# A hybrid decoder trunk on one core: a ring of split weights of four units instead of three, from the first pair of experts on

## The chip, the core and the metric

One core of a Trainium2 chip runs the whole kernel. The metric is the device time of one execution in microseconds (us). TensorE (PE) multiplies, VectorE (DVE) and ScalarE (ACT) work on elements, GpSimd (POOL) has small work, SyncE (SP) issues the loads.

## What is computed

Two decoder layers over 256 tokens of width 1024, in float32. Layer 0 has differential attention, a dense SwiGLU of width 2816 and a gated per-layer embedding. Layer 1 has a pooling mixer, a mixture of eight experts of width 3584 with two experts to a token, and again a gated embedding. The part around the change is the experts:

```python
def swiglu(xn, w_gate, w_up, w_down):
    return (jax.nn.silu(xn @ w_gate) * (xn @ w_up)) @ w_down

def moe_swiglu(xn, w_router, w_gate, w_up, w_down):
    logits = (xn @ w_router).astype(jnp.float32)
    top_v, top_i = lax.top_k(logits, TOP_K)
    top_w = jax.nn.softmax(top_v, axis=-1)
    gates = jnp.sum(jax.nn.one_hot(top_i, N_EXPERTS, dtype=jnp.float32) * top_w[..., None], axis=-2)
    out = jnp.zeros_like(xn)
    for e in range(N_EXPERTS):
        ye = swiglu(xn, w_gate[e], w_up[e], w_down[e])
        out = out + gates[..., e:e + 1].astype(xn.dtype) * ye
    return out
```

The weights of the eight experts are 336 of some 400 units of 1 MiB that the kernel reads.

## The kernel before, in words

**Units.** All weights pass through the core in units of 128 partitions by 2048 float32 (`UNIT`, 1 MiB), counted by one index u. A product in float32 is made of three products in the format fp32r: each weight and each activation is split in a high part (rounded copy) and a low part (rest), and high x high, high x low and low x high are summed (`product`, L342). So a unit goes through four steps:

- SP loads it into one of `RAW` = 7 slots of `raw` (`load`, L331, with the transfer at L340). The load of unit u waits until DVE has split the unit that had the slot, u-7.
- ACT writes the high part into `w_hi` (`split_hi`, L290; the copy is L307). It waits for the landing, and for `unit_used`: PE must have given back the unit that had the same slot of the ring of split weights. `SPLIT` = 3, so unit u waits for u-3.
- DVE writes the low part into `w_lo` (`split_lo`, L309; L324) after ACT, and counts `lo_ready`.
- PE waits for `lo_ready` and multiplies; its last matmul counts `unit_used`.

Each engine runs a list of instructions written out by hand, in order. At step n of a block ACT and DVE issue the split of unit u + n + `AHEAD` (2), and around it the block's small work: the silu (L1521), the high part of the hidden rows (L1526, L1529), its low part (L2076, L2079), the results (`result_hi`, `result_lo`, L2304), their addition to the residual (L2313) and the gathering of tokens for the next experts (`gather_piece` on PE, L1092).

**The expert stage.** The first expert runs alone (`first_turn`, units 56 to 95). Then come pairs of experts (`pair`, unit index from `U_PAIR`), three pairs for these inputs, the third in a loop over a register; then the last expert alone (`last_turn`), its last two down units, and the second layer's embedding gate. Each pair has seven blocks f of 512 hidden columns, and in each block twelve units: two gate, two up and two down units of the one expert, e = 0, and the same of the other, e = 1. Expert e = 0 has at most 64 tokens (`few`): its up and down units take 8 matmuls (`product_few`, L1111 and L1112), all others 12 (L344 to L346). In the first two blocks of a pair results of experts before are scattered and added; in the last one the next experts' tokens are gathered. Twelve units begin with one fold of hidden rows (L929); the stretch from one to the next is called a period here.

**Counting over the turns.** The pair loop reuses the same unit indices: `PER_EXPERT` = 42 units per expert are added as `PER_EXPERT * k` to each wait. 42 and 84 are divisible by 3 and by 7, so slots are the same in each round.

**Space.** Two units of the first expert (87 and 88, `EXTRA`) are loaded ahead into `extra_raw`, outside the ring of `raw`, over the space of an earlier stage. After they have been split this space lies idle.

Of the kernel before, what the change touches and what calls it, by code (L numbers as in the profile page):

```python
# [29 lines left out]
P = 128  # L30
# [41 lines left out]
EXTRA_TURNS = 10  # L72
U_PAIR = U_TURN - 2


def trunk(nc, dram):
    ctx = ExitStack()
    with ctx:
# [14 lines left out]
        with nc.sbuf_tensor("wide", [P, 6144], F32) as wide:  # L93
            pass
        extra_raw = sb("extra_raw", [P, EXTRA * UNIT])
        xb = sb("xb", [P, 2 * D], F32R)
# [171 lines left out]
        def raw_slot(u):  # L268
# [3 lines left out]
            return raw[:, ring(u) % RAW, :]  # L272

        def load_wait(eng, u, k=0):

            if in_wide(u):
                eng.wait_ge(extra_landed[u - U_WIDE], 16)
            else:
                eng.wait_ge(landed[ring(u) % RAW], 16 * (ring(u) // RAW + 1) + 16 * (PER_EXPERT // RAW) * k)

# [9 lines left out]
        def split_hi(u, k=0, by=None):  # L290

            load_wait(nc.scalar, u, k)
            if u == U_POOL:
                nc.scalar.wait_ge(mixer_scaled, 2)
            if u >= SPLIT:
                nc.scalar.wait_ge(unit_used, u - SPLIT + 1 + PER_EXPERT * k)
            if by is not None:
                n, c0 = by
                nc.scalar.wait_ge(gain_cols_landed, 16 * len(COLUMNS))
                for c in range(KD if u == U_POOL else 4):  # L300
                    width = 256 if u == U_POOL else 512
                    cols = slice(width * c, width * c + width)
                    last = nc.scalar.activation(w_hi[:, u % SPLIT, cols], raw_slot(u)[:, cols], ACT.Copy,
                                                scale=column(n, c0 + c))
                last.then_inc(hi_ready, 1)
                return
            nc.scalar.activation(w_hi[:, u % SPLIT, :], raw_slot(u), ACT.Copy).then_inc(hi_ready, 1)  # L307

        def split_lo(u, k=0, by=None):  # L309

            nc.vector.wait_ge(hi_ready, u + 1 + PER_EXPERT * k)
            if by is not None:
                n, c0 = by
                nc.vector.wait_ge(gain_cols_landed, 16 * len(COLUMNS))
                for c in range(KD if u == U_POOL else 4):
                    width = 256 if u == U_POOL else 512
                    cols = slice(width * c, width * c + width)
                    last = nc.vector.scalar_tensor_tensor(out=w_lo[:, u % SPLIT, cols], in0=raw_slot(u)[:, cols],
                                                          scalar=column(n, c0 + c),
                                                          in1=w_hi[:, u % SPLIT, cols].bitcast(F32),  # L320
                                                          op0=ALU.mult, op1=ALU.subtract)
                last.then_inc(lo_ready, 1)
                return
            nc.vector.tensor_tensor(w_lo[:, u % SPLIT, :], raw_slot(u), w_hi[:, u % SPLIT, :].bitcast(F32),  # L324
                                    ALU.subtract).then_inc(lo_ready, 1)

        def split_wait(eng, u, k=0):

            eng.wait_ge(lo_ready, u + 1 + PER_EXPERT * k)
# [18 lines left out]
        def weights(u, c, n0, n, width):  # L348

            at = c * width + n0  # L350
            return w_hi[:, u % SPLIT, at:at + n], w_lo[:, u % SPLIT, at:at + n]

# [9 lines left out]
        def _(sp):  # L362
# [154 lines left out]
            for half, view in enumerate(down_views(e, FB - 1)):  # L517
                load(sp, U_TURN + half, view, turns)
            load_ple(1, U_TURN + 2, turns)

# [114 lines left out]
        def _(pe):  # L635
# [635 lines left out]
            for half in range(2):  # L1271
                down(U_TURN + half, FB - 1, half, JF + FB - 1, 1, turns, end=half == 1, h_t=(a_hi, a_lo))

# [11 lines left out]
            def next_part():  # L1285

                return project_part(1, *next(parts), U_TURN + 2)

            unit(U_TURN + 2, turns)
            next_part()  # L1290
# [12 lines left out]
            last.then_inc(unit_used, 1)  # L1303
            gates(1, U_TURN + 3, turns)


        @block.scalar
        def _(act):
            def used(u, k=0):

                act.wait_ge(unit_used, u + 1 + PER_EXPERT * k)

# [412 lines left out]
            turns = extra + (NE - 1)  # L1725
            pairs = act.value_load(more[0:1, 1:2], min_val=0, max_val=EXTRA_TURNS // 2) + 3
            pair(0, first=True)
            pair(2)
            with act.Fori(3, pairs + 1) as it:
                pair((it - 1) * 2)  # L1730
            last_turn(turns - 1)
            split_hi(U_TURN + AHEAD, turns)
            for n in range(2):
                if n == 0:
                    act.wait_ge(y_half, 1)
                else:
                    used(U_TURN + 1, turns)
                nc.scalar.activation(y_hi[:, 512 * n:512 * n + 512], ps[:, 3 + n, :], ACT.Copy).then_inc(y_hi_ready, 1)

            split_hi(U_TURN + 1 + AHEAD, turns, by=(5, 0))  # L1740
            transposed_hi(5)
            split_hi(U_TURN + 2 + AHEAD, turns, by=(5, 4))
            square_norm(5, turns)
            split_hi(U_TURN + 3 + AHEAD, turns, by=(5, 0))
            split_hi(U_TURN + 4 + AHEAD, turns, by=(5, 4))
            sigmoids(1, 0, U_TURN + 4, turns)
            sigmoids(1, 1, U_TURN + 6, turns, tiles=(0,))
            act.wait_ge(resid_ready, 18)
            for h, bank in enumerate((GATE_BANKS[1][3], GATE_BANKS[1][0])):
                used(U_TURN + 5 + h, turns)  # L1750
                nc.scalar.activation(sig[1][:, 256 * h:256 * h + 256], ps[:, bank, 0:256], ACT.Sigmoid,
# [4 lines left out]
        def _(dve):  # L1756
# [8 lines left out]
            def used(u, k=0):  # L1765

                dve.wait_ge(unit_used, u + 1 + PER_EXPERT * k)

# [607 lines left out]
            def pair(k, slots, first=False):  # L2376

                for f, e in PAIR_BLOCKS:
                    g, u = block_at_seq(f, e), pair_unit(f, e, first)
                    bare = first and f == 0 and e == 0  # L2380
                    for n in range(4 if bare else 6):
                        split_lo(u + n + AHEAD, k)
                        if f == 0 and e == 1 and n == 0 and not first:
# [23 lines left out]
            def last_turn(k):  # L2407

                for f in range(FB):
                    g, u = JF + FB + f, last_unit(f)  # L2410
                    for n in range(6 if f else 8):
                        split_lo(u + n + AHEAD, k)
                        if f == 0 and n == 6:
# [16 lines left out]
            turns = extra + (NE - 1)  # L2430
            pairs = dve.value_load(more[0:1, 1:2], min_val=0, max_val=EXTRA_TURNS // 2) + 3
            pair(0, iota_few[:, :], first=True)
# [4 lines left out]
            split_lo(U_TURN + AHEAD, turns)  # L2437
            for n in range(2):
# [17 lines left out]
            transposed_lo(5, (0,))  # L2456
            split_lo(U_TURN + 1 + AHEAD, turns, by=(5, 0))
            transposed_lo(5, (1, 2, 3))
            split_lo(U_TURN + 2 + AHEAD, turns, by=(5, 4))
            norm_mean(5, 0)  # L2460
            norm_mean(5, 1)
            split_lo(U_TURN + 3 + AHEAD, turns, by=(5, 0))
            split_lo(U_TURN + 4 + AHEAD, turns, by=(5, 4))
            add_gated(1, 0)
# [158 lines left out]
```

## Time and profile before

| | us |
|---|---|
| median of 3 runs | 1371.45 (1371.35 to 1371.47) |
| the profiled execution | 1370.36 |
| its span in the trace | 1368.6 |
| PE busy | 1323.0 |
| DVE busy | 1155.5 |
| ACT busy | 951.6 |

Between the span and the time of the profiled execution lie 1.76 us. The granted clock of TensorE is 1.00 throughout. A matmul of 512 columns is shown with 0.39 us, while the next one starts 0.23 us after it: ends are modelled and overlap, so short idle times of PE do not show in its busy time. PEld is PE's weight load. POOL's spans are rough, and its work here is small. "DMA share" in the windows can be a little above 1 where the packets of an engine overlap.

### The profile page before, as it was taken

What the parts mean: (1) busy time and instruction counts of PE and PEld (TensorE: products, weight loads), DVE (VectorE), ACT (ScalarE), POOL (GpSimd) and SP (SyncE); (2) the same over time, 40 slices, a digit from 0 to 9 for tenths busy, and PEclk for the clock granted to TensorE, in tenths of its full rate; (3) what the DMA queues carried; (4) which work ended last, traced back from release to release, by engine and by line L of the source; (5) the groups of instructions that cost most, each with busy time, mean ns of one, the idle gap of its engine ahead of it and who ended that gap; (6) DMA issues with size and microseconds to landing.
All of it is one profiled execution on the core that took longest, in us unless ns stands there. A gap on an engine that the chain in (4) does not pass through costs nothing.

```text
span 1368.6 us, 17326 instructions
## 1 busy us (share of the span) xinstructions
PE 1323.0 (97%) x6404; PEld 1082.3 (79%) x6404; DVE 1155.5 (84%) x963; ACT 951.6 (70%) x879; POOL 72.3 (5%) x133
## 2 busy tenths in 40 slices
PE   8999999999999999999999999999999999999998
PEld 7776888888877887777777777777777777778887
DVE  6897655556889989999989999898999898899886
ACT  5676544446776777777777777777777777777775
POOL 2120920000200000000000000000000000000000
PEclk9999999999999999999999999999999999999999
DMA  8743765555299899999999999999999999999980
GB/s 302 265 133 92 252 204 193 184 185 166 81 363 335 306 341 359 366 390 394 379 388 354 346 381 382 392 381 391 357 359 362 385 393 389 336 395 368 354 311 31
DMA packets 197860, 422.46 MB, mean 309 GB/s; under 512 B 13064, under 2 KB 37392, under 8 KB 197776
## 3 DMA queue, kind: packets, MB, share of 16 engines
q1 hardware_dynamic: 197776, 421.35, 84.8%
q8 instruction: 52, 0.85, 0.2%
q14 instruction: 32, 0.26, 0.1%
HBM read 420.27 MB, written 1.05 MB: 308 GB/s over the span
## 4 chain that ended last, share of the span: by engine, by line
PE 76%; DVE 15%; ACT 5%; issue 2%; SPq 1%; DMA 1%; POOL 0%; ACTq 0%; DVEq 0%; POOLq 0%
PE ps L344 20%; PE ps L346 19%; PE ps L345 19%; DVE w_lo L324 11%; PE ps L952 5%; ACT w_hi L307 4%; PE ps L950 3%; PE ps L929 1%; PE ps L1092 1%; PE ps L932 1%; PE ps L1105 1%; PE ps L949 1%; PE ps L1111 1%; DMA raw<-in_attn_w_qkv_dram 1%; PE ps L1112 1%
## 5 line engine op out<-in xcount | busy, mean ns | idle before, releaser
L324 DVE TENSOR_TENSOR w_lo<-raw,w_hi 128x2048 fp32r<-128x2048 f32 x382 | 871.1, 2290 | 128.8 <-ACT w_hi L307 125.6
L307 ACT ACTIVATE w_hi<-raw 128x2048 fp32r<-128x2048 f32 x385 | 734.9, 1916 | 223.2 <-PE ps L346 203.6
L344 PE MATMUL ps<-w_hi,xe 128*128 128x512 f32 x392 | 156.3, 399 | 1.7 <-DVE w_lo L324 1.5
L346 PE MATMUL ps<-w_hi,xe 128*128 128x512 f32 x392 | 153.1, 391 | 0.0
L345 PE MATMUL ps<-w_lo,xe 128*128 128x512 f32 x392 | 152.8, 390 | 0.0
L344 PE MATMUL ps<-w_hi,h_t_hi 128*128 128x512 f32 x360 | 141.0, 392 | 2.2 <-DVE w_lo L324 2.2
L345 PE MATMUL ps<-w_lo,h_t_hi 128*128 128x512 f32 x360 | 140.2, 390 | 0.0
L346 PE MATMUL ps<-w_hi,h_t_lo 128*128 128x512 f32 x360 | 140.2, 389 | 0.0
L344 PE MATMUL ps<-w_hi,xb 128*128 128x512 f32 x336 | 135.2, 402 | 4.1 <-DVE w_lo L324 3.5
L346 PE MATMUL ps<-w_hi,xb 128*128 128x512 f32 x336 | 131.3, 391 | 0.0
L345 PE MATMUL ps<-w_lo,xb 128*128 128x512 f32 x336 | 131.0, 390 | 0.0
L952 PE MATMUL ps<-a_all,w_hi 128*128 128x512 f32 x308 | 109.8, 396 | 0.0
L950 PE MATMUL ps<-a_all,w_lo 128*128 128x256 f32 x352 | 90.9, 279 | 0.0
L2507 POOL TENSOR_TENSOR rstd<-mean_sq,minus_half 128x1 f32<-128x1 f32 (+2 forms) x20 | 23.9, 1198 | 1268.7 <-DVE mean_sq L1772 1187.5
L1111 PE MATMUL ps<-w_hi,p_t_hi 128*128 128x512 f32 x168 | 70.3, 418 | 20.0 <-DVE w_lo L324 19.1
L344 PEld LDWEIGHTS ps<-w_hi,xe 128*128 128x128 f32 x392 | 73.7, 188 | 16.7 <-DVE w_lo L324 2.6
L346 PEld LDWEIGHTS ps<-w_hi,xe 128*128 128x128 f32 x392 | 73.6, 188 | 15.9
L345 PEld LDWEIGHTS ps<-w_lo,xe 128*128 128x128 f32 x392 | 73.8, 188 | 14.3
L344 PE MATMUL ps<-w_hi,a_all 128*128 128x512 f32 (+1 forms) x216 | 84.5, 391 | 0.1
L344 PEld LDWEIGHTS ps<-w_hi,xb 128*128 128x128 f32 x336 | 63.1, 188 | 23.7 <-DVE w_lo L324 7.8
L346 PE MATMUL ps<-w_hi,a_all 128*128 128x512 f32 (+1 forms) x216 | 81.9, 379 | 0.0
L345 PE MATMUL ps<-w_lo,a_all 128*128 128x512 f32 (+1 forms) x216 | 81.6, 378 | 0.0
(321 smaller groups left out, 1890.4 us busy)
## 6 DMA issues: line engine op xcount, KB each, us to landing
raw<-in_moe_w_gate_dram SPq DMA_DIRECT2D x112, 1024.0 KB, 7.1
raw<-in_moe_w_up_dram SPq DMA_DIRECT2D x111, 1024.0 KB, 7.4
raw<-in_moe_w_down_dram SPq DMA_DIRECT2D x111, 1024.0 KB, 7.2
raw<-in_attn_w_qkv_dram SPq DMA_DIRECT2D x11, 1024.0 KB, 12.8
raw<-in_ffn_w_gate_dram SPq DMA_DIRECT2D x11, 1024.0 KB, 5.4
raw<-in_ffn_w_up_dram SPq DMA_DIRECT2D x11, 1024.0 KB, 5.4
raw<-in_ffn_w_down_dram SPq DMA_DIRECT2D x11, 1024.0 KB, 5.0
raw<-in_ple_w_gate_dram SPq DMA_DIRECT2D x8, 1024.0 KB, 5.3
```

The costliest lines, as they stand in the source:

```text
L307: nc.scalar.activation(w_hi[:, u % SPLIT, :], raw_slot(u), ACT.Copy).then_inc(hi_ready, 1)
L324: nc.vector.tensor_tensor(w_lo[:, u % SPLIT, :], raw_slot(u), w_hi[:, u % SPLIT, :].bitcast(F32), ALU.subtract).then_inc(lo_ready, 1)
L344: nc.tensor.matmul(out, x[0], w[0], start=first, stop=False)
L345: nc.tensor.matmul(out, x[0], w[1], start=False, stop=False)
L346: return nc.tensor.matmul(out, x[1], w[0], start=False, stop=last)
L929: last = nc.tensor.matmul(ps[:, 2, n * FEW:(n + 1) * FEW], hidden[:, n * P:(n + 1) * P], fold[:, :], start=True, stop=True)
L932: last = nc.tensor.transpose(ps[:, 2, n * P:(n + 1) * P], hidden[:, n * P:(n + 1) * P], ident[:, :])
L949: nc.tensor.matmul(ps[:, bank, :], w[0], a_all[:, :, cols], start=True, stop=False)
L950: last = nc.tensor.matmul(ps[:, bank, 0:SEQ], w[1], a_hi[:, cols], start=False, stop=False)
L952: last = nc.tensor.matmul(ps[:, bank, :], w[0], a_all[:, :, cols], start=False, stop=c == KD - 1)
L1111: nc.tensor.matmul(out, x, w[0], start=first, stop=False)
L2507: return nc.gpsimd.tensor_tensor(rstd[:, at:at + n], mean_sq[:, at:at + n], minus_half[:, 0:n], ALU.pow)
```

## The change

From the first pair on, the ring of split weights has four slots. Slots 0 to 2 are those of `w_hi` and `w_lo`; the fourth is `w_more`, which lies where `extra_raw` was. ACT and DVE split unit u + n + 3 at step n, and wait for the release of the unit four before, so for the same unit of PE as before. `U_PAIR` is moved up by 84 indices, so that the units of the pairs have indices of their own (178 and up, 180 to 261 in the first pair), and `rounds` takes these 84 off in each count. 84 is divisible by 4 as well. The last expert's last units get the indices from `U_TAIL`, with the register one turn lower. The two splits that had stood ahead of the loops' lead (`U_PAIR + 2 + AHEAD` on each of ACT and DVE) are issued before the first pair, and the one after the last expert's turn goes into that turn. The diff, cut to its core (each change of `split_lo` mirrors that of `split_hi`; the calls of the tail replace `U_TURN + n, turns` by `U_TAIL + n, turns - 1`):

```diff
-U_PAIR = U_TURN - 2
+U_PAIR = U_TURN - 2 + 2 * PER_EXPERT
+U_TAIL = U_PAIR + 2 + PER_EXPERT
+DEEP = SPLIT + 1
...
-        extra_raw = sb("extra_raw", [P, EXTRA * UNIT])
+        with nc.sbuf_tensor("extra_raw", [P, EXTRA * UNIT], F32) as extra_raw:
+            pass
+        w_more = sb("w_more", [P, 2, UNIT], F32R)
...
+        def rounds(u, k):
+
+            return PER_EXPERT * k - (2 * PER_EXPERT if u >= U_PAIR else 0)
+
+        def split_at(u):
+
+            if u >= U_PAIR:
+                at = u % DEEP
+                return (w_more[:, 0, :], w_more[:, 1, :]) if at == SPLIT else (w_hi[:, at, :], w_lo[:, at, :])
+            return w_hi[:, u % SPLIT, :], w_lo[:, u % SPLIT, :]
...
             if u >= SPLIT:
-                nc.scalar.wait_ge(unit_used, u - SPLIT + 1 + PER_EXPERT * k)
+                deep = u >= U_PAIR and not (isinstance(k, int) and k == 0 and u < U_PAIR + 2 + SPLIT)
+                nc.scalar.wait_ge(unit_used, u - (DEEP if deep else SPLIT) + 1 + rounds(u, k))
+            hi = split_at(u)[0]
...
-            nc.scalar.activation(w_hi[:, u % SPLIT, :], raw_slot(u), ACT.Copy).then_inc(hi_ready, 1)
+            nc.scalar.activation(hi, raw_slot(u), ACT.Copy).then_inc(hi_ready, 1)
...
             if u >= RAW:
                 before_it = ring(u) - RAW
-                split_wait(eng, before_it if before_it < U_WIDE and u < U_PAIR else before_it + EXTRA, k)
+                before_it += EXTRA if before_it >= U_WIDE else 0
+                eng.wait_ge(lo_ready, before_it + 1 + rounds(u, k))
...
                     for n in range(4 if first and f == 0 and e == 0 else 6):
-                        split_hi(u + n + AHEAD, k)
+                        split_hi(u + n + AHEAD + 1, k)
...
                     for n in range(6 if f else 8):
-                        split_hi(u + n + AHEAD, k)
+                        split_hi(u + n + AHEAD + 1, k)
...
+            split_hi(U_PAIR + 2 + AHEAD)
             pair(0, first=True)
...
             last_turn(turns - 1)
-            split_hi(U_TURN + AHEAD, turns)
```

## Rows read from the trace of the kernel before

**Rows 1.** The page: busy time by engine, and DMA over 40 equal slices

```profile
PE 1323.0 (97%) x6404; PEld 1082.3 (79%) x6404; DVE 1155.5 (84%) x963; ACT 951.6 (70%) x879; POOL 72.3 (5%) x133
...
DMA  8743765555299899999999999999999999999980
```

**Rows 2.** Waits from 500 to 1200 us: us in total, times, longest us

```profile
PE ps L1111 <- DVE w_lo L324: 19.1, 37, 1.2
PE ps L344 <- DVE w_lo L324: 3.5, 11, 0.8
...
DVE w_lo L324 <- ACT w_hi L307: 58.3, 110, 1.2
...
ACT w_hi L307 <- PE ps L346: 153.2, 165, 1.7
```

**Rows 3.** PE in order of time, short units of one period: start us, us

```profile
704.21 0.39 PE L1112 MATMUL ps<-w_lo,xe 128*128 128x512 f32 x1
705.36 0.50 PE L1111 MATMUL ps<-w_hi,p_t_hi 128*128 128x512 f32 x1 [0.77 <-DVE w_lo L324]
705.70 0.39 PE L1112 MATMUL ps<-w_lo,p_t_hi 128*128 128x512 f32 x1
...
707.09 0.39 PE L1112 MATMUL ps<-w_lo,p_t_hi 128*128 128x512 f32 x1
707.65 0.50 PE L1111 MATMUL ps<-w_hi,p_t_hi 128*128 128x512 f32 x1 [0.17 <-DVE w_lo L324]
...
709.37 0.39 PE L1112 MATMUL ps<-w_lo,p_t_hi 128*128 128x512 f32 x1
709.85 0.50 PE L344 MATMUL ps<-w_hi,xb 128*128 128x512 f32 x1
```

**Rows 4.** Windows of a period each, then of twenty: last columns PE clock, DMA share, GB/s

```profile
646.82:679.21 32.39, 31.36 (x142) 25.08 (x140) 29.25 (x17) 24.30 (x16) 0.00 (x0) 1.00 1.03 384
711.56:748.06 36.50, 35.19 (x174) 28.82 (x173) 32.13 (x25) 26.84 (x25) 0.00 (x0) 1.00 0.97 354
748.06:783.19 35.13, 33.31 (x151) 27.04 (x150) 33.78 (x23) 26.24 (x19) 0.00 (x0) 1.00 0.99 356
783.19:816.95 33.76, 32.75 (x148) 26.20 (x147) 31.64 (x21) 24.44 (x17) 0.00 (x0) 1.00 1.01 376
...
1084.46:1117.23 32.77, 31.32 (x141) 25.09 (x140) 30.05 (x21) 24.52 (x17) 0.00 (x0) 1.00 1.04 394
...
514.24:1181.99 667.75, 644.41 (x2917) 517.92 (x2916) 611.02 (x375) 500.34 (x344) 0.00 (x0) 1.00 1.01 376
```

**Rows 5.** DMA from 20 to 50 us: 40 slices, issues with us to landing

```profile
GB/s 106 225 339 350 291 216 322 355 393 399 391 388 374 377 388 388 388 391 388 380 385 391 388 388 391 388 380 385 391 382 393 391 385 382 385 393 391 388 382 257
...
raw<-in_attn_w_qkv_dram SPq DMA_DIRECT2D x7, 1024.0 KB, 13.2
```

**Rows 6.** GB/s in 40 slices: 679.21 to 711.56 us, then 711.56 to 748.06

```profile
GB/s 393 291 370 393 365 291 377 390 403 408 405 398 410 425 400 370 400 390 362 385 395 398 387 390 387 387 387 387 385 385 393 380 400 415 380 415 375 408 327 357
...
GB/s 404 308 352 415 393 382 404 395 382 386 397 413 417 400 404 422 391 379 382 182 83 312 406 420 359 382 325 88 227 400 402 292 413 426 166 242 426 408 388 402
```

**Rows 7.** DMA issues from 500 to 1200 us: KB each, median us to landing

```profile
raw<-in_moe_w_gate_dram SPq DMA_DIRECT2D x82, 1024.0 KB, 7.4
```

**Rows 8.** Groups from 679.21 to 711.56 us: busy, mean ns, idle before

```profile
L324 DVE TENSOR_TENSOR w_lo<-raw,w_hi 128x2048 fp32r<-128x2048 f32 x13 | 29.6, 2289 | 3.1 <-ACT w_hi L307 3.0
L307 ACT ACTIVATE w_hi<-raw 128x2048 fp32r<-128x2048 f32 x13 | 24.8, 1916 | 8.2 <-PE ps L346 7.0 <-PE ps L1112 1.2
```

**Rows 9.** Window of the last expert's turn, columns as in rows 4

```profile
1216.00:1300.00 84.00, 83.39 (x378) 68.50 (x377) 78.01 (x49) 60.85 (x41) 0.00 (x0) 1.00 1.00 367
```

**Rows 10.** The chain that ended last, one fold: start us, us

```profile
712.87 0.84 PE ps L929 x8
```

**Rows 11.** ACT and DVE in order of time, small work of a period

```profile
702.89 0.58 ACT L1521 ACTIVATE tmp<-ps 128x512 f32<-128x512 f32 x1
...
709.71 0.68 DVE L2071 TENSOR_TENSOR tmp<-tmp,ps 128x512 f32<-128x512 f32 x1
```

More of the change, by code:

```diff
@@ L278, in load_wait @@
             else:
-                eng.wait_ge(landed[ring(u) % RAW], 16 * (ring(u) // RAW + 1) + 16 * (PER_EXPERT // RAW) * k)
+                eng.wait_ge(landed[ring(u) % RAW], 16 * (ring(u) // RAW + 1) + 16 * (rounds(u, k) // RAW if isinstance(k, int) else PER_EXPERT // RAW * (k - 2)))
         def pick_of(e, tt):
@@ L302, in split_hi @@
                     cols = slice(width * c, width * c + width)
-                    last = nc.scalar.activation(w_hi[:, u % SPLIT, cols], raw_slot(u)[:, cols], ACT.Copy,
+                    last = nc.scalar.activation(hi[:, cols], raw_slot(u)[:, cols], ACT.Copy,
                                                 scale=column(n, c0 + c))
@@ L306, in split_hi @@
                 return
-            nc.scalar.activation(w_hi[:, u % SPLIT, :], raw_slot(u), ACT.Copy).then_inc(hi_ready, 1)
+            nc.scalar.activation(hi, raw_slot(u), ACT.Copy).then_inc(hi_ready, 1)
         def split_lo(u, k=0, by=None):
-            nc.vector.wait_ge(hi_ready, u + 1 + PER_EXPERT * k)
+            nc.vector.wait_ge(hi_ready, u + 1 + rounds(u, k))
+            hi, lo = split_at(u)
             if by is not None:
@@ L317, in split_lo @@
                     cols = slice(width * c, width * c + width)
-                    last = nc.vector.scalar_tensor_tensor(out=w_lo[:, u % SPLIT, cols], in0=raw_slot(u)[:, cols],
+                    last = nc.vector.scalar_tensor_tensor(out=lo[:, cols], in0=raw_slot(u)[:, cols],
                                                           scalar=column(n, c0 + c),
-                                                          in1=w_hi[:, u % SPLIT, cols].bitcast(F32),
+                                                          in1=hi[:, cols].bitcast(F32),
                                                           op0=ALU.mult, op1=ALU.subtract)
@@ L323, in split_lo @@
                 return
-            nc.vector.tensor_tensor(w_lo[:, u % SPLIT, :], raw_slot(u), w_hi[:, u % SPLIT, :].bitcast(F32),
+            nc.vector.tensor_tensor(lo, raw_slot(u), hi.bitcast(F32),
                                     ALU.subtract).then_inc(lo_ready, 1)
         def split_wait(eng, u, k=0):
-            eng.wait_ge(lo_ready, u + 1 + PER_EXPERT * k)
+            eng.wait_ge(lo_ready, u + 1 + rounds(u, k))
         def load(eng, u, view, k=0):
@@ L350, in weights @@
             at = c * width + n0
-            return w_hi[:, u % SPLIT, at:at + n], w_lo[:, u % SPLIT, at:at + n]
+            hi, lo = split_at(u)
+            return hi[:, at:at + n], lo[:, at:at + n]
         def acts(c, tt):
@@ L517, in _ @@
             for half, view in enumerate(down_views(e, FB - 1)):
-                load(sp, U_TURN + half, view, turns)
-            load_ple(1, U_TURN + 2, turns)
+                load(sp, U_TAIL + half, view, turns - 1)
+            load_ple(1, U_TAIL + 2, turns - 1)
             out = dram["out"][0].rearrange("(t p) d -> p t d", p=P)
@@ L1271, in _ @@
             for half in range(2):
-                down(U_TURN + half, FB - 1, half, JF + FB - 1, 1, turns, end=half == 1, h_t=(a_hi, a_lo))
+                down(U_TAIL + half, FB - 1, half, JF + 2 * FB - 1, 1, turns - 1, end=half == 1, h_t=(a_hi, a_lo))
             def last_scatter(n, tt):
@@ L1285, in next_part @@
             def next_part():
-                return project_part(1, *next(parts), U_TURN + 2)
-            unit(U_TURN + 2, turns)
+                return project_part(1, *next(parts), U_TAIL + 2)
+            unit(U_TAIL + 2, turns - 1)
             next_part()
@@ L1303, in _ @@
             last.then_inc(unit_used, 1)
-            gates(1, U_TURN + 3, turns)
+            gates(1, U_TAIL + 3, turns - 1)
         @block.scalar
@@ L1309, in used @@
             def used(u, k=0):
-                act.wait_ge(unit_used, u + 1 + PER_EXPERT * k)
+                act.wait_ge(unit_used, u + 1 + rounds(u, k))
             scratch = [tmp[:, 512:1024], tmp[:, 1024:1536], tmp[:, 1536:2048], xe[:, 0:512]]
@@ L1736, in _ @@
                 else:
-                    used(U_TURN + 1, turns)
+                    used(U_TAIL + 1, turns - 1)
                 nc.scalar.activation(y_hi[:, 512 * n:512 * n + 512], ps[:, 3 + n, :], ACT.Copy).then_inc(y_hi_ready, 1)
-            split_hi(U_TURN + 1 + AHEAD, turns, by=(5, 0))
+            split_hi(U_TAIL + 1 + AHEAD, turns - 1, by=(5, 0))
             transposed_hi(5)
-            split_hi(U_TURN + 2 + AHEAD, turns, by=(5, 4))
+            split_hi(U_TAIL + 2 + AHEAD, turns - 1, by=(5, 4))
             square_norm(5, turns)
[L1744 to L1747, printed above, removed]
+            split_hi(U_TAIL + 3 + AHEAD, turns - 1, by=(5, 0))
+            split_hi(U_TAIL + 4 + AHEAD, turns - 1, by=(5, 4))
+            sigmoids(1, 0, U_TAIL + 4, turns - 1)
+            sigmoids(1, 1, U_TAIL + 6, turns - 1, tiles=(0,))
             act.wait_ge(resid_ready, 18)
             for h, bank in enumerate((GATE_BANKS[1][3], GATE_BANKS[1][0])):
-                used(U_TURN + 5 + h, turns)
+                used(U_TAIL + 5 + h, turns - 1)
                 nc.scalar.activation(sig[1][:, 256 * h:256 * h + 256], ps[:, bank, 0:256], ACT.Sigmoid,
@@ L1765, in used @@
             def used(u, k=0):
-                dve.wait_ge(unit_used, u + 1 + PER_EXPERT * k)
+                dve.wait_ge(unit_used, u + 1 + rounds(u, k))
             def norm_mean(n, tt):
@@ L2381, in pair @@
                     for n in range(4 if bare else 6):
-                        split_lo(u + n + AHEAD, k)
+                        split_lo(u + n + AHEAD + 1, k)
                         if f == 0 and e == 1 and n == 0 and not first:
@@ L2411, in last_turn @@
                     for n in range(6 if f else 8):
-                        split_lo(u + n + AHEAD, k)
+                        split_lo(u + n + AHEAD + 1, k)
                         if f == 0 and n == 6:
@@ L2431, in _ @@
             pairs = dve.value_load(more[0:1, 1:2], min_val=0, max_val=EXTRA_TURNS // 2) + 3
+            split_lo(U_PAIR + 2 + AHEAD)
             pair(0, iota_few[:, :], first=True)
@@ L2436, in _ @@
             last_turn(turns - 1)
-            split_lo(U_TURN + AHEAD, turns)
             for n in range(2):
@@ L2456, in _ @@
             transposed_lo(5, (0,))
-            split_lo(U_TURN + 1 + AHEAD, turns, by=(5, 0))
+            split_lo(U_TAIL + 1 + AHEAD, turns - 1, by=(5, 0))
             transposed_lo(5, (1, 2, 3))
-            split_lo(U_TURN + 2 + AHEAD, turns, by=(5, 4))
+            split_lo(U_TAIL + 2 + AHEAD, turns - 1, by=(5, 4))
             norm_mean(5, 0)
             norm_mean(5, 1)
-            split_lo(U_TURN + 3 + AHEAD, turns, by=(5, 0))
-            split_lo(U_TURN + 4 + AHEAD, turns, by=(5, 4))
+            split_lo(U_TAIL + 3 + AHEAD, turns - 1, by=(5, 0))
+            split_lo(U_TAIL + 4 + AHEAD, turns - 1, by=(5, 4))
             add_gated(1, 0)
```

## The prediction, made before the changed kernel was run

> **What bounds the kernel now.** I began with the page. TensorE (PE) is busy 97% of the span, VectorE (DVE) 84%, ScalarE (ACT) 70%, and from the twelfth slice on the DMA row is 9 almost throughout [rows 1]. So three resources are near their limit in the expert stage, and the question is which takes over when one stops holding the others up. The change acts there, from the first pair of experts on, some 500 to 1200 us.
>
> The waits of that stretch name the present brake. PE waited 48 times, 22.6 us, for a `w_lo` of DVE; DVE 110 times, 58.3 us, for a `w_hi` of ACT; ACT 165 times, 153.2 us, for PE's 12-matmul units, which is the ring of split weights: unit u+2 is split when PE has given back unit u-1 [rows 2]. No wait of ACT for a transfer stands in that list.
>
> The order of time shows where it bites [rows 3]. A unit of the small expert has 8 matmuls, 1.83 us at 0.23 us from start to start; a unit of the other has 12, 2.74 us. From PE's release to a finished split there are 1.92 us on ACT and 2.29 on DVE [rows 8], with small gaps 4.3 us. Two units of lead cover 4.3 us when units are long (5.5 us), not when they are short (3.7 us). So PE starts at 705.36 where 704.44 was due, at 707.65 instead of 707.32 and at 709.85 instead of 709.60: 0.92, 0.33 and 0.25 us, and each stall costs another 0.1 us in the next gap (0.33 or 0.34 for 0.23). That is 1.8 us in this period of twelve units. By the totals: a stall shows 0.39 - 0.23 = 0.16 us too short, since the end of a matmul is modelled, and 0.1 follows it: 22.6 + 48 x 0.26 = 35 us, and a few stalls shorter than 0.16 us, which do not show as idle, make it 35 to 40. This is all that a longer ring can win at PE.
>
> The windows by period give the other two [rows 4]. There are 21 periods, seven to a pair; four of seven are plain, 32.4 to 32.8 us, and three carry results and gathers, 36.50, 35.13 and 33.76 us. DVE is busy 29.25 us of a plain one, but 33.78 of the 35.13. DMA moves 12.58 MB in each (twelve units of 1 MiB).
>
> **What the transfers can do.** In the early stage seven loads stood in the queue at once, each landing after 13.2 us, and the rate lay at 380 to 393 GB/s, mostly 388 [rows 5]. So 388 GB/s is what this queue gives when it is never short of work, and a period of twelve units then takes 12.58 MB / 388 = 32.4 us. A plain period lasts just that, at 370 to 410 GB/s in most slices; the one with the gather, 36.50 us, shows holes of 83 and 88 GB/s [rows 6]. I read this as: in plain periods the transfers are already full, in the others they wait for released buffers. Over the 20 periods from 514.24 to 1181.99, 667.75 us at 376 GB/s, 251.7 MB moved [rows 4]. Full all along, they would take 648.7 us at 388, 638.8 at 394 (the best plain period) and 655.5 at 384 (the poorest of the undisturbed ones).
>
> The Trainium skill ("DMA: Bandwidth & Descriptors", Measured) gives 425 GB/s for one core streaming 16 MB; by that the period would need 29.6 us of transfer and the full PE gain would come. Its specifications also say that about 358 GB/s binds from HBM, which would be 35.1 us a period and leave nothing to win. The plain periods, at 384 to 394 GB/s, are above the second; nothing of this trace reaches the first for long.
>
> **The change part by part.** *No instruction is added or removed*: the same 250 splits of the pairs, by 1.92 and 2.29 us each, in the same order on ACT, DVE and PE. The waits of `split_hi` fire at the same PE event, release of u-1; only what is split then is one unit further on. Cost zero.
>
> *The lead* grows from two units to three: 3 x 1.83 = 5.5 us against 4.3, so the short run no longer stalls by latency. Backlog: in the short run (two up, two down units, 7.3 us) DVE owes four splits, 9.2 us plus 0.68 for the hidden rows [rows 11]; the third unit of lead and the long units before and after (2.74 against 2.29) repay that. Gain at PE 35 to 40 us, less the period where DVE is full: 33.78 against 35.13 - 2.1 = 33.0, 0.8 us twice, and small gaps. Call it 33 if nothing else held.
>
> *The bookkeeping*: the two splits taken out of the loop ahead of the pairs and out of the tail are issued at nearly the same place in order; the one that moves into the last expert's loop had stood right behind it. Zero, at most one 1.92 us ACT split either way in the tail, if it met the eviction of the last result.
>
> *The space*: the fourth slot lies over the two units loaded ahead (units 87 and 88), which are split long before slot four is first written, behind the release of unit 95. No new wait that is late. Zero.
>
> *The loads*: seven raw slots as before, and each load still follows the split of the unit seven before. A slot's cycle is 7 x 2.70 = 18.9 us; 7.4 is flight [rows 7], 4.5 splitting, so a landed unit lies about 7 us. Once splits stop waiting for PE, that stock is drawn on.
>
> *The sum.* The 20 periods go from 667.75 to 648.7 us if no hole is left: 19 us. Holes that no released buffer would close (queue work between pairs, uneven landings) I take at a quarter of that, 5 us. Against it, the stock of 7 us is spent once: 4 us more, since late landings then reach PE and ACT keeps its order. 19 - 5 + 4 = 18 us. The ends: 10 (384 GB/s, nothing of the stock, 2 us of holes) and 28 (394 GB/s and 29 us of gain, the same 5 off, 4 on). First expert, dense stage and last expert's turn stay: the last turn has long units and is busy already, 83.4 of 84 us [rows 9]. The profiled execution took 1370.36 us, its span 1368.6; minus 18 it is 1352.4, and as the median of the runs lies 1.09 above it, 1353.5 us.
>
> **Rivals.**
> - *Transfers have room.* If queued loads went faster than at the start (down projections come in longer rows; slices of 410 to 420 occur in plain periods), the PE figure holds: 33 us, 1338 us. For it: ACT never waits for a landing now. Against: the even rates of plain periods and the 9s of the page [rows 1, 6]. Chance 0.12.
> - *Transfers yield nothing more.* The 355 GB/s of the busy periods is what they can do beside that work; only the plain holes of the gather close, about 2 us in two of the three pairs, plus part of the stock: 7 us, 1364 us. Chance 0.13.
> - *No effect*, if the limit were in DVE's order (hidden rows and results behind splits), so that one more unit of lead is never filled: 1371 us. Against: DVE idles 3.1 us of a plain period, for ACT [rows 8]. Chance 0.03.
> - *Slower.* ACT now stands at the split of u+3 until it has landed, and the silu and the hidden copy, 0.58 us each, are queued behind; DVE's 0.68 and PE's fold, 0.84, follow [rows 10, 11]. If a late landing exposed that chain in every period, PE would lose 0.58 + 0.58 + 0.68 + 0.84 = 2.7 us for the 1.8 removed: 0.9 x 21 = 19 us, 1390 us. It decides from 1.8 us of exposed chain per period on; but hidden rows are wanted only five units later, so I give it 0.03.
> - *PE's clock.* It stood at 1.00 in the last turn at 99% busy [rows 9]; no case of its own.
>
> **How the numbers follow.** Chances: forecast 0.69, room 0.12, nothing more 0.13, no effect 0.03, slower 0.03. About 0.2% (2.7 us) is what can be told from no change. The first three are faster: 0.94; same 0.03; slower 0.03. The forecast's own range is 1343.5 to 1361.5; I stretch it to 1344 to 1362, which leaves out 0.12 for room, half of "nothing more" and the two last: 2 in 10.
>
> **What would show it.** Right: the waits of PE for `w_lo` in short units almost gone; ACT waiting tens of us for `raw`, where it waited for none; landings at 10 us or more, not 7.4; 385 to 390 GB/s in all periods; the early ones of the first pair at 30.5 to 31, the later plain ones back at 32.4, with the three others at about 34.5, 34 and 32.5. Wrong: plain periods at 30.6 throughout (transfers had room), or GB/s unchanged with PE stalls gone elsewhere (DVE or order binds).

## The result, and the profile after

The changed kernel takes 1337.66 us (median of 4 runs, 1337.33 to 1338.38), the kernel before in the same comparison 1371.4. The ratio is 0.9757, 95% interval 0.974 to 0.9774: 33.7 us less. The forecast was 1353.5, with a range from 1344 to 1362, so the direction was right and the size was missed by 16 us. The measured time is the one that the rival "transfers have room" gave, 1338 us.

The page of the changed kernel: span, busy times, and the DMA lines over 40 slices.

```profile
span 1336.1 us, 17325 instructions
PE 1307.6 (98%) x6404; PEld 1084.0 (81%) x6404; DVE 1151.2 (86%) x963; ACT 950.5 (71%) x879; POOL 72.3 (5%) x133
...
GB/s 305 259 129 97 246 202 191 189 192 169 127 257 342 362 300 365 368 395 394 394 394 394 395 394 393 394 394 394 394 388 394 394 394 394 386 394 394 369 279 32
```

The same work is done in 32.5 us less span (1368.6 us before). From the eighteenth to the thirty-seventh slice the rate is 393 to 395 GB/s, but for two slices (388 and 386). The forecast had taken 388 for the limit.

The windows of the changed kernel: a plain period, the three that carry gathers and results, and the same twenty periods as before (last columns: granted clock, DMA share, GB/s).

```profile
639.89:670.44 30.55, 30.55 (x141) 25.18 (x140) 29.32 (x17) 23.79 (x16) 0.00 (x0) 1.00 1.05 394
701.22:735.57 34.35, 34.19 (x172) 28.71 (x171) 32.20 (x25) 28.33 (x26) 0.00 (x0) 1.00 1.04 395
735.57:770.12 34.55, 33.16 (x151) 27.04 (x150) 33.44 (x23) 26.13 (x19) 0.00 (x0) 1.00 1.04 394
770.12:801.95 31.83, 31.83 (x147) 26.36 (x146) 31.65 (x21) 24.17 (x17) 0.00 (x0) 1.00 1.04 394
...
515.37:1150.50 635.13, 629.59 (x2913) 520.50 (x2914) 605.06 (x373) 495.62 (x343) 0.00 (x0) 1.00 1.04 392
```

Against [rows 4]: 30.55 us for 32.39, 34.35 for 36.50, 34.55 for 35.13, 31.83 for 33.76, and the twenty together 635.13 for 667.75. So 32.6 us of the gain lie in these twenty periods. In a plain period PE is busy all of the 30.55 us. The one with the most work on VectorE won least, 0.6 us, as forecast (it had 34 us for it).

Waits in the changed kernel, 500 to 1170 us (us in total, times, longest us).

```profile
PE ps L949 <- DVE tmp L2091: 3.0, 5, 2.1
PE ps L1125 <- DVE y_lo L2324: 2.9, 2, 1.5
PE ps L363 <- DVE w_lo L342: 0.8, 2, 0.5
...
ACT w_hi L324 <- PE ps L365: 76.1, 83, 2.6
ACT w_more L324 <- PE ps L365: 24.5, 31, 1.1
ACT w_hi L324 <- DMA raw<-in_moe_w_down_dram: 12.2, 23, 0.7
ACT w_hi L324 <- DMA raw<-in_moe_w_up_dram: 11.8, 16, 0.9
```

PE's 22.6 us of waits for `w_lo` [rows 2] have shrunk to 0.8. In their place stand waits for small work: L949 is the fold, which waits for the product with the silu, and L1125 the scatter, which waits for a result's low part. ACT now waits for landings, where it waited for none; these and the smaller rows of that kind make 41 us over 69 waits, little of which reaches PE (experiment 4).

### The profile page after: what moved, and what is told of

Same layout as the page of the kernel before. It is cut to its first block, busy times and chain, and to the rows that moved or that the text cites. A ratio compares the mean times of both kernels' runs of the same rounds, so it can differ in the third digit from the quotient of the medians.

```text
span 1336.1 us, 17325 instructions
## 1 busy us (share of the span) xinstructions
PE 1307.6 (98%) x6404; PEld 1084.0 (81%) x6404; DVE 1151.2 (86%) x963; ACT 950.5 (71%) x879; POOL 72.3 (5%) x133
## 3 DMA queue, kind: packets, MB, share of 16 engines
HBM read 420.27 MB, written 1.05 MB: 315 GB/s over the span
## 4 chain that ended last, share of the span: by engine, by line
PE 77%; DVE 10%; DMA 7%; ACT 3%; issue 2%; SPq 1%; POOL 0%; DVEq 0%; ACTq 0%; POOLq 0%
PE ps L363 18%; PE ps L365 18%; PE ps L364 18%; DMA raw<-in_moe_w_gate_dram 6%; PE ps L972 5%; DVE w_lo L342 4%; PE ps L1132 3%; PE ps L1131 3%; PE ps L970 3%; ACT w_hi L324 2%; DVE w_more L342 1%; PE ps L949 1%; PE ps L1112 1%; PE ps L1125 1%; PE ps L952 1%
## 5 line engine op out<-in xcount | busy, mean ns | idle before, releaser
L342 DVE TENSOR_TENSOR w_lo<-raw,w_hi 128x2048 fp32r<-128x2048 f32 x308 | 703.2, 2292 | 88.8 <-ACT w_hi L324 88.0
L324 ACT ACTIVATE w_hi<-raw 128x2048 fp32r<-128x2048 f32 x311 | 592.9, 1916 | 150.8 <-PE ps L365 117.1
L342 DVE TENSOR_TENSOR w_more<-raw,w_more 128x2048 fp32r<-128x2048 f32 x74 | 169.4, 2289 | 11.1 <-ACT w_more L324 10.7
L324 ACT ACTIVATE w_more<-raw 128x2048 fp32r<-128x2048 f32 x74 | 142.0, 1919 | 42.9 <-PE ps L365 32.4
L363 PE MATMUL ps<-w_hi,xe 128*128 128x512 f32 x284 | 111.8, 394 | 1.6 <-DVE w_lo L342 1.5
L365 PE MATMUL ps<-w_hi,xe 128*128 128x512 f32 x284 | 110.7, 390 | 0.0
L364 PE MATMUL ps<-w_lo,xe 128*128 128x512 f32 x284 | 110.6, 389 | 0.0
L363 PE MATMUL ps<-w_hi,xb 128*128 128x512 f32 x252 | 100.8, 400 | 0.9 <-DVE w_lo L342 0.8
L365 PE MATMUL ps<-w_hi,xb 128*128 128x512 f32 x252 | 98.4, 391 | 0.0
L363 PEld LDWEIGHTS ps<-w_hi,h_t_hi 128*128 128x128 f32 x348 | 65.3, 188 | 15.9 <-DVE w_lo L342 3.1
L365 PEld LDWEIGHTS ps<-w_hi,h_t_lo 128*128 128x128 f32 x348 | 65.3, 188 | 13.8
L364 PEld LDWEIGHTS ps<-w_lo,h_t_hi 128*128 128x128 f32 x348 | 65.4, 188 | 13.2
```

Of the source, the lines that this page charges most:

```text
L324: nc.scalar.activation(hi, raw_slot(u), ACT.Copy).then_inc(hi_ready, 1)
L342: nc.vector.tensor_tensor(lo, raw_slot(u), hi.bitcast(F32), ALU.subtract).then_inc(lo_ready, 1)
L363: nc.tensor.matmul(out, x[0], w[0], start=first, stop=False)
L364: nc.tensor.matmul(out, x[0], w[1], start=False, stop=False)
L365: return nc.tensor.matmul(out, x[1], w[0], start=False, stop=last)
```

## The experiments

Each timed run is compared with the kernel before on the same chip. Ratios are given with their 95% intervals. Differences from the changed kernel are taken across chips, except in experiment 11; there it took 1338.13 us, here 1337.66.

**1. Back to the old lead.** All of the edit but the lead and the splits that were moved for its sake:

```diff
-                nc.scalar.wait_ge(unit_used, u - (DEEP if deep else SPLIT) + 1 + rounds(u, k))
+                nc.scalar.wait_ge(unit_used, u - SPLIT + 1 + rounds(u, k))
...
-                        split_hi(u + n + AHEAD + 1, k)
+                        split_hi(u + n + AHEAD, k)
```

> The changed kernel with the old lead: the four slots, the new unit numbers and the new place stay, but a split again waits for the unit three before and is issued two units ahead. If the lead is what wins, this is back at the time before, 1371 us within 1.5, with PE's 48 waits for w_lo and 22 us back and landings at 7.4 us. If something else of the edit wins (the numbers, the place of the fourth slot), it stays below 1360.

Measured: 1371.18 us, ratio 1.0003 (0.9993 to 1.0012). PE waits again, in three groups where there were two, since the fourth slot has a name of its own (500 to 1200 us):

```profile
PE ps L1131 <- DVE w_lo L342: 12.9, 19, 1.0
PE ps L1131 <- DVE w_more L342: 6.2, 18, 1.2
PE ps L363 <- DVE w_lo L342: 3.5, 11, 0.8
```

Together 22.6 us, the sum of before. The new numbering and the place of the fourth slot cost and bring nothing; all of the gain comes with the lead. The moved splits went back together with the lead here, so this run does not price them by themselves.

**2. The free slot without the new place in the lists.**

```diff
-                        split_hi(u + n + AHEAD + 1, k)
+                        split_hi(u + n + AHEAD, k)
...
-            split_hi(U_PAIR + 2 + AHEAD)
             pair(0, first=True)
```

with the same on VectorE, and the tail's first split back behind the last turn. The wait for the unit four before stays.

> The changed kernel with the ring of four but the old place in the lists: step n of ACT and DVE issues the split of u+n+2, which waits only for the release of the unit four before. Theory 1 (the free slot is what counts): ACT reaches the split earlier anyway, since its waits for PE go, and most of the gain stays, 1338 to 1350 us. Theory 2 (the place in the list counts: the silu and the hidden copies ahead of a split wait for PE, so that a split cannot run more than two units ahead): most of the gain is lost, 1360 to 1371 us.

Measured: 1334.72 us, ratio 0.9738 (0.9722 to 0.9755). Theory 1 holds and more: this version came out below the expected 1338 to 1350, and below the changed kernel. Beside it on one chip, with five rounds (experiment 11 below), it took 1335.16 against 1338.13.

**3. and 4. A sixth of the bytes less, before and after.** Down units of the pairs load half; products of their other half run on stale data.

```diff
+            if cut:
+                dst, view = dst[:, 0:1], view[:, 0:1]
             eng.dma_start(dst, view).then_inc(landed[ring(u) % RAW], 16)
```

> The kernel before, but each down unit of the three pairs loads only its first half (84 of 250 units at 0.5 MiB, a sixth of the bytes less); all splits and products stay, on stale data in the second half. My prediction read the plain periods as full of transfers: then a period falls from 32.4 towards PE's own pace, and 5 to 15 us are won, 1356 to 1366 us. If PE's wait for the splits alone sets the pace before, nothing changes: 1371 us within 1.5, and plain periods of 32.4 us at some 325 GB/s.

Measured: 1371.34 us, ratio 1.0003 (0.9994 to 1.0013). A plain period of this run:

```profile
679.10:711.50 32.40, 31.36 (x141) 25.09 (x141) 29.32 (x17) 24.55 (x17) 0.00 (x0) 1.00 0.93 326
```

The same 32.40 us at 326 GB/s as at 384. That decides against the reading on which the forecast rests.

> The changed kernel with the same cut of a sixth of the bytes. If the transfers, at 394 GB/s all along, now set the pace, the waits of ACT for landings (41 us) go and the time falls by 4 to 10 us, to 1328 to 1334 us, down to where PE has no idle. If PE is the bound already and the transfers only keep up with it, it stays at 1337.7 within 1.5 us.

Measured: 1335.77 us, ratio 0.9746 (0.973 to 0.9762), 1.9 us below the changed kernel: between the two expectations, less than the 4 to 10 of "transfers set the pace". The intervals of the two ratios overlap, so the totals alone hardly show it. The periods show where it lies. In the changed kernel the last plain period of the second pair runs from the first to the second of these folds:

```profile
895.34 1.00 PE L949 MATMUL ps<-fold,tmp 128*128 128x64 f32 x8
926.97 1.10 PE L949 MATMUL ps<-fold,tmp 128*128 128x64 f32 x8 [0.28 <-DVE tmp L2091]
```

That is 31.63 us. The same period takes 30.78 us in the first pair and 31.90 in the third, and 30.43 us in all three with a sixth fewer bytes. So PE sets the pace nearly everywhere, and the transfers cost some 3 us of this trace at the ends of the pairs.

**5. and 6. Where the transfers' floor lies.** PE's work is cut: the low-by-high product is left out in two gate units of each period; then the bytes are cut too.

```diff
+                    if n == 0 and x is xb:
+                        last = product_few(ps[:, n, :], x[:, 2 * d * P:(2 * d + 1) * P], w, d == 0, d == KD - 1)
-                    if few and n == 1:
+                    elif few and n == 1:
```

> The changed kernel, with the low-by-high product left out in the two gate units of the second expert of each pair: PE has 2 x 4 matmuls of 0.23 us less in each of the 21 periods, 1.8 us each, 39 us in all; loads and splits stay. If the transfers at 394 GB/s are a floor that the changed kernel has nearly reached (639 us for 20 periods, less the stock of landed units), at most 3 us are won: 1334 to 1338. If PE is still the only bound, some 25 to 39 us are won, as far as VectorE allows: 1299 to 1313.

Measured: 1339.65 us, ratio 0.9767 (0.9751 to 0.9784). Some 39 us of PE's work went and nothing was won; at 2 us above the changed kernel it is even outside the expected 1334 to 1338. Two plain periods, and two waits from the lists for 500 to 1170 us:

```profile
672.80:704.70 31.90, 29.66 (x133) 23.50 (x132) 29.34 (x17) 24.78 (x17) 0.00 (x0) 1.00 1.04 394
897.00:928.90 31.90, 29.65 (x133) 23.50 (x132) 29.32 (x17) 24.75 (x17) 0.00 (x0) 1.00 1.04 394
...
PE ps L949 <- DVE tmp L2093: 18.1, 18, 3.0
ACT w_hi L324 <- DMA raw<-in_moe_w_up_dram: 24.8, 32, 0.9
```

Part of this time is the clock's. In the profiled execution (1341.03 us) PE stood idle for 2.53 us before 745.03; from 746 to 749 us the granted clock was 0.50, the lower of its two levels (1.2 GHz), and this period took 36.44 us, where its like in the next pair, at 1.00 throughout, took 34.89. The same happened from 518 to 524 us, after an idle time of 3.02 us. The two executions of this run with the highest mean clock (0.997) took 1338.7 and 1338.8 us.

> The same cut of PE's work, and a sixth of the bytes of the pairs less. If the transfers were what held the run before this one, the time now falls towards VectorE's pace (busy 29.3 us of a plain period, 33.8 in the one with results): 1315 to 1328 us. If something else held it (VectorE or the order of the lists), it stays where the run with all bytes was.

Measured: 1320.31 us, ratio 0.9635 (0.9619 to 0.9651), and a plain period falls to this:

```profile
881.60:910.90 29.30, 28.88 (x134) 23.74 (x133) 28.82 (x17) 24.18 (x17) 0.00 (x0) 1.00 1.00 357
```

So the transfers do have a floor, 31.9 us for twelve units at 394 GB/s, and not 32.4. The product of the two numbers shows nothing (12.58 MB in 31.9 us are 394 GB/s whatever holds them up); what shows it is that ACT waits for landings in run 5, 63 us in the four longest rows of that kind, that no such wait is left in run 6, and that 19 us go with the bytes. The changed kernel's plain periods, 30.55 us, go below the floor for a while on landed units.

The fold's wait for the silu product grows from 3.0 us in the changed kernel to 18.1 in run 5. On VectorE this product is queued behind a split, and in run 5 that split can be late because its unit has not landed. But in run 6, where ACT waits for no landing, the fold still waits 12.7 us. So by this comparison only 5.4 of the 18.1 us are the landings'. Where the rest comes from is not shown; PE, with less work, may simply be early at the fold.

**7. and 8. Fewer raw slots in effect.** In the pairs a load waits for the split of the unit six before (changed kernel), or five before (kernel before).

```diff
-                eng.wait_ge(lo_ready, before_it + 1 + rounds(u, k))
+                eng.wait_ge(lo_ready, before_it + early + 1 + rounds(u, k))
```

> The changed kernel with one raw slot less in effect: in the pairs a load waits for the split of the unit six before it, not seven. If the stock of landed units carried the changed kernel through (7 us in the kernel before, 0.5 us left at the end now), a unit less of it costs about its 2.7 us, less what PE's own idle covers: 1338.5 to 1341. If transfers play no part, 1337.7 within 1.5.

Measured: 1343.64 us, ratio 0.9801 (0.9785 to 0.9818): 6.0 us more than the changed kernel, where 0.8 to 3.3 were expected. The last two plain periods of the first and of the second pair:

```profile
641.10:672.30 31.20, 31.20 (x143) 25.48 (x143) 29.22 (x17) 24.08 (x17) 0.00 (x0) 1.00 1.04 394
672.30:704.30 32.00, 31.31 (x142) 25.09 (x141) 29.30 (x17) 24.76 (x17) 0.00 (x0) 1.00 1.04 394
867.50:898.70 31.20, 31.06 (x142) 25.15 (x140) 29.15 (x17) 24.59 (x16) 0.00 (x0) 1.00 1.04 393
898.70:930.60 31.90, 31.23 (x141) 25.08 (x140) 29.33 (x17) 24.77 (x17) 0.00 (x0) 1.00 1.04 394
```

The last one of each pair is back at the floor; in the third pair it takes 31.90 us too. The stock is not spent once: the three slow periods of a pair (in the changed kernel 34.35 + 34.55 + 31.83 = 100.7 us, for 95.8 us of transfers) fill it by 4.9 us, and the plain ones draw on it. The changed kernel itself reaches the floor with its last plain period in the second and third pair (experiment 4), so there was nothing to spare, and a slot less is paid about 2 us in each of three pairs.

> The kernel before with two raw slots less in effect in the pairs. Its landed units wait about 7 us for ScalarE, two units are 5.4 us, so most periods should stay at 32.4 and the total within 3 us of 1371; the landing times should fall towards 6 us and the rate of transfers stay what PE consumes. If the 384 to 390 GB/s of its plain periods were the queue's limit, a thinner queue would cost at once, 10 us and more.

Measured: 1370.04 us, ratio 0.9997 (0.9987 to 1.0006). The total is unchanged: before, two of seven raw slots were not needed. The faster landings that the expectation names did not come (7.5 us, 7.4 to 7.6 before): as much was under way in the queue as before.

**9. A shorter split in the kernel before.** Ring of three; the splits of the three units that PE waited for are done in halves, so that VectorE starts after ScalarE's first half.

```diff
+                nc.scalar.activation(w_hi[:, u % SPLIT, 0:1024], raw_slot(u)[:, 0:1024], ACT.Copy).then_inc(part_ready, 1)
+                nc.scalar.activation(w_hi[:, u % SPLIT, 1024:2048], raw_slot(u)[:, 1024:2048], ACT.Copy).then_inc(hi_ready, 1)
```

> The kernel before, ring of three, lead of two. Only the splits of the three units that PE used to wait for in each period (steps 2 to 4 of the small expert's block, 18 to a pair) are done in halves: VectorE starts on the first half while ScalarE does the second, so that release to finished split takes about 1.0 + 2.4 us and gaps, 3.5 us, where it took 4.3; two short units are 3.7 us. If the latency of the split against two short units is what the kernel before loses, most of its 1.8 us per period go, in 18 of 21 periods: 1340 to 1352 us. If the stall is VectorE's backlog in the short run, halves (0.14 us more each) make it no better: 1370 to 1374.

Measured: 1365.79 us, ratio 0.9963 (0.9951 to 0.9974): 5.5 us instead of 20 to 30, and so between the two expectations. PE and then VectorE of this run, in order of time:

```profile
671.61 0.50 PE L1128 MATMUL ps<-w_hi,p_t_hi 128*128 128x512 f32 x1 [0.43 <-DVE w_lo L324]
673.88 0.50 PE L1128 MATMUL ps<-w_hi,p_t_hi 128*128 128x512 f32 x1 [0.15 <-DVE w_lo L324]
...
666.39 2.29 DVE L341 TENSOR_TENSOR w_lo<-raw,w_hi 128x2048 fp32r<-128x2048 f32 x1 [0.43 <-ACT w_hi L312]
668.60 0.68 DVE L2096 TENSOR_TENSOR h_t_lo<-ps,h_t_hi 128x512 fp32r<-128x512 f32 x1
669.20 6.89 DVE L324 TENSOR_TENSOR w_lo<-raw,w_hi 128x1024 fp32r<-128x1024 f32 x6
676.01 0.67 DVE L2088 TENSOR_TENSOR tmp<-tmp,ps 128x512 f32<-128x512 f32 x1
```

VectorE had 0.43 us of idle before a long unit's split, and then works without a gap through the short ones. The latency is not the brake any more, VectorE's rate is: 2.3 us a split against 1.83 us of PE. The trace of the kernel before had shown nearly as much. VectorE there, in the period of [rows 3]:

```profile
702.03 0.68 DVE L2079 TENSOR_TENSOR h_t_lo<-ps,h_t_hi 128x512 fp32r<-128x512 f32 x1
703.02 6.78 DVE L324 TENSOR_TENSOR w_lo<-raw,w_hi 128x2048 fp32r<-128x2048 f32 x3 [0.30 <-ACT w_hi L307]
```

Three splits stand in a row without a gap, behind an idle time of 0.30 us (0.30 to 0.32 in the other plain periods). As VectorE does no less work in halves, they can hardly win more than this idle time: 0.3 us in each of 18 periods, 5.4 us. Measured were 5.5.

**10. Less work for VectorE.** As run 9, but of the second half of those three low parts one column is written, the rest left out.

```diff
-                    cols = slice(1024 * at, 1024 * at + 1024)
+                    cols = slice(1024 * at, 1024 * at + (1 if at else 1024))
```

> The run in halves won 5.5 us where 20 to 30 were expected, and in its trace VectorE works without a gap through the short units (six halves, 6.9 us for 5.5 us of PE). Here VectorE leaves out the second half of those three low parts in a period (one column of it is done, so that the counts stay); ScalarE's part, the ring of three and all waits are the same, so the low parts of these columns are stale. If VectorE's rate in the short run, with no idle time saved up before it, is what the kernel before loses to, PE's waits for w_lo nearly all go and the time is 1338 to 1350 us. If it is the chain from release to split by ScalarE's latency, the time stays near 1365.

Measured: 1338.71 us, ratio 0.9756 (0.9739 to 0.9772). With a ring of three, taking 1.0 us of VectorE's work from each of three units per period wins what the fourth slot wins. The low part is also finished 1.0 us sooner here, so this run changes the latency too and does not separate rate from latency by itself; what separates them is that VectorE had no idle time left to win in run 9. VectorE now has idle time in the short run, as these rows show, and PE's waits for `w_lo` from 500 to 1200 us are down to 5.1 us:

```profile
664.14 1.28 DVE L324 TENSOR_TENSOR w_lo<-raw,w_hi 128x1024 fp32r<-128x1024 f32 x2
666.06 1.29 DVE L324 TENSOR_TENSOR w_lo<-raw,w_hi 128x1024 fp32r<-128x1024 f32 x2 [0.64 <-ACT w_hi L309]
667.95 1.29 DVE L324 TENSOR_TENSOR w_lo<-raw,w_hi 128x1024 fp32r<-128x1024 f32 x2 [0.59 <-ACT w_hi L309]
```

**11. The faster version, beside the changed kernel.** Run 2's kernel again, the changed kernel itself, and run 2's with a sixth of the bytes less, on one chip.

> The ring of four with the old place in the lists again, on one chip with the changed kernel and with more rounds: 1334.7 us within 1, 3 us below the changed kernel. PE no longer waits 2.1 and 2 x 1.5 us for the silu product and the results behind a split.

> The changed kernel itself, unchanged, for the comparison with the run before this one: 1337.7 us within 1.

> The ring of four with the old place in the lists, a sixth of the bytes of the pairs less. With all bytes this version took 1334.7 us. If transfers cost it as little as they cost the changed kernel (1.9 us), 1332 to 1334; if the late landings at the end of each pair hold it more, 1328 to 1331.

Measured: 1335.16 us (1334.5 to 1337.03; ratio 0.974, 0.9727 to 0.9753), 1338.13 us (1336.7 to 1341.54; 0.9756, 0.9743 to 0.9769) and 1333.89 us (0.9733, 0.9718 to 0.9748). The medians of the first two differ by 3.0 us, as they did in the runs before (1334.72 and 1337.66), but the intervals overlap; the version with the old place in the lists is probably 2 to 3 us faster. Its trace says why. Waits of PE, 500 to 1170 us, in run 2's kernel, second time:

```profile
PE ps L1131 <- DVE w_more L342: 1.9, 2, 0.9
PE ps L363 <- DVE w_lo L342: 1.2, 4, 0.6
```

The waits of the fold and of the scatter are gone, 5.9 us, and 2.3 us for splits are new. In this version the silu product and the result's low part stand one place earlier in the lists, ahead of a split that is not urgent. With a sixth fewer bytes it takes 1.3 us less, which is within the noise (the intervals overlap).

## Why the prediction was wrong

**What bounds the kernel before: half right.** PE's stalls in the short units were the brake, and the total by the waits, 35 to 40 us with about 33 to be won, was right: 33.7 were. The figure was added up from PE's waits and holds whatever caused them, which is why it could come out although the cause was read wrongly (below). It stood in the text as "if nothing else held".

**The step that failed is the transfers' limit, 388 GB/s, and the period of 32.4 us worked out from it.** I saw a plain period last 32.4 us and move 12.58 MB, and read the agreement with 388 GB/s as a limit. It was the demand: PE's stalls made the period, and the transfers followed. The sum was built on the transfers as the bound, and the bound was PE. Run 3 shows it, with the same 32.40 us at a sixth fewer bytes. The plateau at the start, 380 to 393 [rows 5], belongs to the attention's weights, whose loads are shaped like the gate and up units; about five of them were under way at once and not seven (13.2 us at 388 GB/s are 5.1 MB). The mix of two thirds gate and up and one third down units got 394, and in [rows 6] the slices of 400 to 425 stood in view. That the longer rows of the down units make the difference is not shown. The floor was there (run 5, 31.9 us), but 0.5 us lower per period: 251.7 MB at 394 are 638.8 us, not 648.7. That is 10 of the 14.6 us by which the twenty periods differ from the sum (32.6 for 18).

**Holes, 5 us: about 3.** The changed kernel moved 249.0 MB in its twenty periods, 392 GB/s; at 394 that is 632 us of the 635.13. This is 2 us of the difference.

**Stock, 4 us once: about 7, and the picture was wrong.** The 251.7 MB that twenty periods use are 2.7 MB more than the 249.0 moved in them, 7 us at 394 GB/s, which is the last 3 us of the difference. And the stock is not only spent: it is filled and drawn on in every pair (run 7), which is why periods of 30.5 to 30.9 us could follow one another in all three pairs. The forecast had the later plain ones back at 32.4; only the last one of the second and of the third pair came near the floor, 31.63 and 31.90.

**Parts at zero: right for numbering and space** (run 1, 1.0003); the moved splits were not priced alone. The period with results did win little. Landings rose to 12 us, ACT waits for them, and the three special periods came out at 34.35, 34.55 and 31.83, near the 34.5, 34 and 32.5 named. "Plain periods at 30.6 throughout" was named as the sign that transfers had room, and it came but for the two near the floor. In the chances, what lies outside the range adds up to 0.245, a quarter, where the text says 2 in 10.

**Why PE stalled: right place, wrong mechanism.** The forecast had 4.3 us from release to split against 3.7 us of two short units. Run 9 separates the two: a shorter latency with the same work on VectorE wins 5.5 us, just the 0.3 us per period in which VectorE waited at the start of the short run. With less work for it besides, run 10 wins 33. In the short run VectorE needs 2.3 us a unit and PE 1.83, so it falls behind; in the long units it has time (0.43 us each), which a full ring of three does not let it use. The fourth slot is a place to put work done in that time. VectorE's idle of 3.1 us in a plain period [rows 8] went to 1.2. The forecast had this shortfall among its terms ("Backlog", 9.2 + 0.68 us against 7.3), but as a side matter that the lead repays, and not as the cause.

**Rivals.** "Nothing more", "no effect" and "slower" are out. "Transfers have room" gave the time, but the room was small: 30.55 us of a plain period lie below the floor of 31.9. ACT standing at a split that has not landed does occur, and in run 5 by the comparison with run 6 it costs PE some 5 us at the fold. In the changed kernel it costs little (experiment 4).

The Trainium skill's 425 GB/s for one core streaming ("DMA: Bandwidth & Descriptors", Measured) was not reached: 394 to 395 held over hundreds of us with four and more units in flight (12 us at 394 GB/s are 4.7 MB). Nor does the 358 of that page's specifications bind here; 394 is above it.

## What to carry to other kernels

That a stretch moves as many bytes as a queue seems to give is no sign of a limit. Look for an engine that waits for a landing: where there is none, the transfers only follow. Or take bytes away and see whether the period changes. When short and long pieces alternate, the producer's rate in the short run counts, and a deeper ring can win at most the time that the producer is idle in the long run (here 3.1 us a period, of which 1.9 were used). The deeper ring needed free slots and not a new place in the hand-written lists: moving the split ahead of the small work probably lost 2 to 3 us of the gain.

## What was not expected of the hardware

- The queue gave 394 GB/s through nearly the whole stage of the changed kernel (landings after 12 us), and the same in the plain periods of run 7 with one unit less under way (10.4 us). The 376 of the kernel before is what it asked for, 251.7 MB in 667.75 us, and no measure of what a queue with landings after 7.4 us can give. I had taken part of its uneven rates (354 to 394) for the memory's own.
- In run 5 landings came after 13 us, and the last two plain periods of each of the three pairs took 31.84 to 31.91 us: where transfers bind, they bind as evenly as an engine does.
- In run 5 idle times of PE of 2.5 and 3.0 us were followed by a granted clock of 0.50 for 3 to 6 us. The executions of run 6 go in the order of their mean clock, from 1315.70 us at 0.998 to 1323.05 us at 0.992.
- Splitting one 2048-column copy into two of 1024 cost little: 1.05 us each on ScalarE against 1.92 whole, 1.21 on VectorE against 2.29.
